# The down weights of sixteen experts in eight ring pieces of 2816 floats in place of eleven of 2048

## The reference, cut to what matters

```
D_MODEL = 1024
N_EXPERTS = 16
EC_CAPACITY = 2
D_FF = 128 * ((8 * D_MODEL // 3 + 127) // 128)    # 2816
```

## Time and profile before

| | |
|---|---|
| runs | 2968.31, 2967.54, 2962.93 us; median 2967.54 us |
| profiled execution | 2965.82 us, span 2964.0 us |
| TensorE matmuls | 2557.9 us busy, 86% of the span, 19787 instructions |
| TensorE weight loads | 1410.3 us busy, 48% |
| VectorE, ScalarE, GpSimd | 888.7, 413.0, 85.2 us busy |
| transfers | 789.18 MB, mean 266 GB/s |
| granted TensorE clock | 0.92 of full over the span |

### The profile page before, as it was taken

The page is one execution under the profiler, slowest core; times in us unless marked ns, Lnnn a source line. Parts: engine busy times, 40 slices in busy tenths (PEclk is TensorE's granted clock), DMA queues, the critical chain, the costliest instruction groups (busy, mean ns, idle before and its releaser), DMA issues. The chain is left out here.

```text
span 2964.0 us, 43931 instructions
## 1 busy us (share of the span) xinstructions
PE 2557.9 (86%) x19787; PEld 1410.3 (48%) x19787; DVE 888.7 (30%) x1788; ACT 413.0 (14%) x810; POOL 85.2 (3%) x93
## 2 busy tenths in 40 slices
PE   6979579988999998999999999879677889779995
PEld 4534235333344443544344443337565878445553
DVE  1216632201212212131303131026538441242222
ACT  1022100200101001021202121013113221000001
POOL 0001000000000000000000000000000200000000
PEclk9988688999999999999999999989878989889998
DMA  5316236799999998899988899863010005259996
GB/s 177 123 48 223 92 130 239 294 382 380 392 379 373 380 421 360 334 375 409 371 360 355 371 407 386 368 263 126 2 37 1 3 7 199 99 240 419 422 422 281
DMA packets 136340, 789.18 MB, mean 266 GB/s; under 512 B 18241, under 2 KB 20553, under 8 KB 65881
## 3 DMA queue, kind: packets, MB, share of 16 engines
q1 hardware_dynamic: 132697, 773.78, 64.9%
q0 software_dynamic: 3456, 12.58, 1.1%
HBM read 774.79 MB, written 11.53 MB: 265 GB/s over the span
## 5 line engine op out<-in xcount | busy, mean ns | idle before, releaser
L3015 PE MATMUL bank<-ring,arena 128*34 128x512 f32 (+1 forms) x3072 | 699.2, 595 | 105.1 <-DMA ring<-in_w_up 75.6
L3015 PEld LDWEIGHTS bank<-ring,arena 128*34 128x34 f32 x3072 | 185.0, 116 | 521.6 <-issue 506.9
L3037 PE MATMUL bank<-ring,arena 128*34 128x512 f32 x1408 | 320.5, 595 | 0.7 <-DVE arena L2021 0.6
L3037 PEld LDWEIGHTS bank<-ring,arena 128*34 128x34 f32 x1408 | 88.0, 112 | 178.2 <-issue 157.0
L303 PE MATMUL bank<-arena,ring 128*128 128x256 f32 (+1 forms) x688 | 158.7, 393 | 3.9 <-DVEq L2038 1.8
L303 PEld LDWEIGHTS bank<-arena,ring 128*128 128x128 f32 x688 | 133.8, 195 | 29.3 <-DVEq L2038 2.2
L3493 PE MATMUL bank<-ring,arena 128*64 128x256 f32 x992 | 111.3, 379 | 4.6 <-DMA ring<-in_moe_w_up 3.9
L2014 DVE TENSOR_TENSOR arena<-arena,bank 34x512 f32<-34x512 f32 x96 | 56.7, 646 | 152.6 <-ACT arena L1086 152.2
L2913 PEld LDWEIGHTS bank<-arena 64*64 64x64 f32 x2304 | 75.4, 139 | 52.6 <-issue 52.1
L313 PE MATMUL bank<-ring,arena 128*128 128x512 f32 (+1 forms) x224 | 98.8, 596 | 0.0
L3493 PEld LDWEIGHTS bank<-ring,arena 128*64 128x64 f32 x992 | 73.4, 137 | 46.3 <-issue 14.4
(11 more groups left out here) (634 smaller groups left out, 3003.6 us busy)
## 6 DMA issues: line engine op xcount, KB each, us to landing
ring<-in_w_gate SPq DMA_DIRECT2D x128, 1408.0 KB, 11.3
ring<-in_w_up SPq DMA_DIRECT2D x128, 1408.0 KB, 12.5
ring<-in_w_down SPq DMA_DIRECT2D x176, 1024.0 KB, 8.6
ring<-in_w_in SPq DMA_DIRECT2D x46, 1024.0 KB, 7.1
ring<-in_moe_w_down SPq DMA_DIRECT2D x33, 1024.0 KB, 15.8
ring<-in_moe_w_gate SPq DMA_DIRECT2D x31, 1024.0 KB, 14.3
ring<-in_moe_w_up SPq DMA_DIRECT2D x31, 1024.0 KB, 17.2
ring<-in_ada_w SPq DMA_DIRECT2D x24, 1024.0 KB, 6.6
```

What stands on the lines that cost most here:

```text
L3015: last = mm(ps[c][row:row + CAP, 0:n], xsT[:, e, k, :], w[:, at:at + n], start=k == 0, stop=k == KT - 1)
L3037: last = mm(ps[6][row:row + CAP, :], hidT[:, 2 * j + f, :], w[:, f, half * BANK:(half + 1) * BANK], start=j + f == 0, stop=j == FT // 2 - ...
```

## The change

The down weights of an expert go over in eight pieces of 2816 floats per partition, as large as a gate or up piece. Partition p now holds 22 consecutive rows of `w_down`, 22 p to 22 p + 21, and piece m is floats 2816 m to 2816 m + 2815 of that line of 22528. With this:

- `DOWN_AT` places eight pieces: one behind k = 2, 3, 5 and 7, two behind k = 4 and 6.
- The transposed hidden column g takes the hidden columns 22 p + g: a step of 22 floats.
- A piece holds 5.5 banks of 512 output columns, so half the piece ends fall in the middle of a bank, and that matmul is cut in two of 256 columns. An expert has 48 down matmuls in place of 44.
- In HBM a piece's 128 lines of 11264 bytes lie 90112 bytes apart. Before, a piece was one closed stretch of 1 MB.

```
-        DOWN_AT = {2: (0, 1), 3: (1, 3), 4: (3, 5), 5: (5, 7), 6: (7, 9), 7: (9, 11)}
-        hid_by2 = hid.rearrange("p (j q f) -> p j f q", q=P, f=2)
+        DOWN_AT = {2: (0, 1), 3: (1, 2), 4: (2, 4), 5: (4, 5), 6: (5, 7), 7: (7, 8)}
+        N_DOWN = FT * D // PIECE
+        hid_by22 = hid.rearrange("p (q j) -> p j q", j=FT)
...
-            for j in range(lo, hi):
-                w = A["w_down"][e][2 * j * P:(2 * j + 2) * P, :]
-                down_pieces[e].append(piece(w.rearrange("(p k) c -> p k c", k=2), 2 * D, "p (k c) -> p k c", {"k": 2}))
+            rows = A["w_down"][e].rearrange("(p j) c -> p (j c)", j=FT)
+            for m in range(lo, hi):
+                down_pieces[e].append(piece(rows[:, m * PIECE:(m + 1) * PIECE], PIECE, "p (o c) -> p (o c)", {"o": 1}))
...
-                    last = mm(ps[6][:, f * CAP:(f + 1) * CAP], hid_by2[0:CAP, g // 2, g % 2, :], ident[:CAP, :CAP],
+                    last = mm(ps[6][:, f * CAP:(f + 1) * CAP], hid_by22[0:CAP, g, :], ident[:CAP, :CAP],
...
-                for j in range(lo, hi):
-                    w, slot, count, _ = down_pieces[e][j]
+                for m in range(lo, hi):
+                    w, slot, count, _ = down_pieces[e][m]
                     pe.wait_ge(slot, count)
-                    for f in range(2):
-                        for row in (0, SLOT):
-                            half = row // SLOT
-                            last = mm(ps[6][row:row + CAP, :], hidT[:, 2 * j + f, :], w[:, f, half * BANK:(half + 1) * BANK],
-                                      start=j + f == 0, stop=j == FT // 2 - 1 and f == 1)
+                    at = m * PIECE
+                    while at < (m + 1) * PIECE:
+                        j, half, c = at // D, at % D // BANK, at % BANK
+                        n = min(BANK - c, (m + 1) * PIECE - at)
+                        row = SLOT * half
+                        last = mm(ps[6][row:row + CAP, c:c + n], hidT[:, j, :], w[:, at - m * PIECE:at - m * PIECE + n],
+                                  start=j == 0, stop=j == FT - 1)
+                        at += n
                     last.then_inc(piece_used, up(piece_used))
```

More of the change, by code:

```diff
@@ L531, in build @@
                         context_pieces[name] = column_pieces(A["w_in_2"], c0, cols)
-        add_down_pieces(N_EXP - 1, 0, FT // 2)
+        add_down_pieces(N_EXP - 1, 0, N_DOWN)
         n_experts = len(pieces)
@@ L3092, in _ @@
                 pe.wait_ge(hid_turned, due(pe, hid_turned))
-            down_pe(N_EXP - 1, 0, FT // 2)
+            down_pe(N_EXP - 1, 0, N_DOWN)
             pe.wait_ge(banks_read, due(pe, banks_read, 2))
```

## The result

The changed kernel takes 3063.82 us, the median of four runs (3056.98 to 3071.49), against 2967.93 us before: a ratio of 1.0323, 95% interval 1.0292 to 1.0354. It is slower, as forecast, but by 96 us and not by 53, and it lies just above the range of 2985 to 3062 us. The profiled execution took 3056.98 us with a span of 3055.0 us, 91.0 us more than before's.

What follows compares the result with a forecast made beforehand. Each expert was taken as a TensorE-bound part, then a transfer-bound part. +67.6 (transposes) - 27.9 (ring) + 0.9 (cuts) + 12.2 (clock) = +52.8 us on 2965.8 us gave 3018.6, with the runs' median 3020 us; range 2985 to 3062 us.

Steps and rivals of the forecast that it cites:

- the part that TensorE bounds: Each expert from k = 0 to the end of `gate_up_pe` of k = 2; work added here adds to the time in full.
- the ring's gain: At the k = 2 release the ring holds 0.786 MB more, 1.86 us less waiting per expert: -27.9 us over 15 experts.
- the part that the transfers bound: Each expert from the end of k = 2 until the next k = 0 pieces land; more TensorE work here is hidden.
- the transposes: Hidden-column transposes at step 22: 704 weight loads at 0.096 us more each, +67.6 us, bounds 0 and +84.5 us.
- the clock: Longer transpose groups make TensorE's clock fall more often, 1.63 us a fall: +12.2 us, bounds 0 and +48.9 us.
- the down products: Cut down matmuls hide in transfer waits, except in the last expert: +0.9 us, bounds 0 and +14 us.
- 0.117 and 0.213 us apart: Start spacing of successive transpose weight loads at steps 2 and 8, the latter taken for step 22: 0.096 us more per load.
- The signs named: In the changed profile, transpose loads near 313 ns median and a group of 22 about 4.8 us in place of 2.66.
- One further fall in every second expert: Clock falls behind transpose groups, counted as 15 x 0.5 x 1.63 = +12.2 us.
- the price per instruction: Down matmuls: 0.214 us per further instruction, lost only where two cut halves for the same rows meet.
- Scattered lines: Rival: down-piece lines 90112 bytes apart in HBM slow the transfers, +23 us, 3043 us in all; chance 0.07.
- The clock's rival: The clock falls behind every transpose group, up to +48.9 us, ending at 3057 us; chance 0.12.

Runs made afterwards that it cites:

- the ladder: The kernel before with its old pieces, its half groups of transposes taking steps of 1, 2, 3, 4, 8, 16 and 22 floats in turn: 3031.03 us, single run.
- Long groups of cheap loads: The kernel before with each transpose done twice at the old step of 2 floats: 3110.45 us, ratio 1.0475.
- The five slots: Kernel with eight pieces and the hidden tile stored in reading order, SP allowing five pieces instead of six in the experts' stage: 3008.7 us, ratio 1.0172.
- closed stretches: The changed kernel with each down piece read from one closed stretch of 1408 KB of w_down: 3061.35 us, ratio 1.0329.

## Why the prediction was right in sign and too small

The stage was read rightly: transposes in the part that TensorE bounds, the ring's gain in the part that the transfers bound, and the two add, as the two halves of the change run alone showed (+129 and -31 us for +96). The sum had three losses too small, the transposes, the clock and the down products, and the gain too small as well. On the profiled spans the miss is 91.0 - 52.8 = 38.2 us: 18.3 from the transposes, 19.2 from the down products and 11.5 from all other matmuls, less the 10.8 us by which TensorE's time without work fell further than the forecast had it (38.7 against 27.9).

- **The transposes: forecast +67.6 us, measured +85.9.** The step that failed is the spacing of slow loads, "0.117 and 0.213 us apart", taken from the first two of a sequence. Over 22 loads the spacing is 0.241 us. The bound of 0.120 us per load, +84.5 us, was nearly the answer. The signs named, a median of 313 ns and 4.8 us for the loads of a group, came out as 337 ns and 5.40 us. That a step of 22 costs what a step of 8 costs held in the ladder (0.245 and 0.241 us), and with it the rule of the Trainium skill (Advanced Engine Details and Errata, SBUF Cachelines) that one access per line is penalised and two are not. The cheaper step of 16 (0.220 us) isn't explained by it.
- **The clock: forecast +12.2 us, measured some +36 to +47 where the step is the only difference.** "One further fall in every second expert" failed. It was read from one expert, with one fall in two groups; before, 22 of the 32 groups have one, and now all 32, mostly longer. The work that the step doesn't touch grew by 47.2 us where the step came alone; with the new pieces it is 2169.8 us at step 22 against 2566.5 - 92.0 - 340.6 = 2133.9 us at step 2, +35.9 us. This was the forecast's own rival, with a chance of 0.12 and a price of up to 48.9 us. Long groups of cheap loads did the same (+43.4 us), so it was the length of the group that decided. Against before the growth is only 23.7 us, since the profile with new pieces and old step has fewer falls (18 of 32) and 12.2 us less of such work. These sums move between profiles: in the kernel with four cut matmuls the same sum is 2573.6 - 91.1 - 321.1 = 2161.4 us, 15 us above before without a cause in the code, so each is good to perhaps 15 us.
- **The ring: forecast -27.9 us, measured -31 us** for the new pieces alone, down products included. That the two lie so close is partly luck. In that profile TensorE's time without work fell by 36.4 us (406.1 to 2936.2 - 2566.5 = 369.7), while the down products took 20.1 us more and the other matmuls 12.2 us less. With the step of 22 the waits fell by 39.8 us, more than 27.9. The five slots bear out the arithmetic of the lead for the waits, 49.2 us for a piece less, not for the time.
- **The down products: forecast +0.9 us, measured +20.1 us of busy time.** The step that failed is the price per instruction, 0.214 us for each in turn, with a loss only where two cut halves meet. Four cut matmuls per expert with such meetings cost 0.6 us in all. The rows fit another count: the instructions of one half of the output rows run one after another, the two halves beside each other, and the fuller half sets the time. By the earlier trace rows one more instruction in each half costs (3.60 - 1.89) / 4 = 0.4275 us, with a tail of 1.89 - 1.71 = 0.18 us. A piece of 5.5 banks has three banks for one half and two and a half for the other, two instructions each. At k = 2 that is 6 x 0.4275 + 0.18 = 2.75 us (measured 2.74); at k = 4, with six banks against five, 5.31 us (5.32); at k = 6, where two pieces make 5.5 banks for each half, 4.88 us (4.89). Balanced, they would take 2.53, 4.88 and 4.88 us. Over k = 2 to 7 the excess is some 1.3 us an expert, 19 us over 15 experts, nearly all of the 20.1. No run changed the order within a piece alone, so this rests on the rows. The work lies in the transfer part, and the waits there gave up 11.9 us more than the lead explains (39.8 against 27.9); that the longer down products took these from them is an inference.
- **Scattered lines** were rightly held unlikely: 426 GB/s, and no difference with closed stretches.
- **The range** ended at 3062 us. With the sustained spacing (+85.9) and both falls (+48.9) the forecast's own terms would have given 2967.5 + 85.9 - 27.9 + 0.9 + 48.9 = 3075 us. The clock's rival was priced alone, on the forecast's transposes, though the two go together: a slower load is what makes the group longer.

## What to carry to other kernels

A layout that gives transfers one closed line can take it from the engine that reads across. Look at the step in floats of every operand loaded as weights, and where it passes two, turn the data on the write of an engine with time to spare. In a group of matmuls that is bound by its loads, count the slower load times all loads and then the clock behind the group: take them as one mechanism, not as two chances, and count falls of the clock over all groups, not in one example. Where matmuls alternate between two halves of output rows, sum each half by itself; the fuller one sets the time. With a ring of slots, what counts is the bytes that it holds when the transfers become the bound, so pieces of full slot size are worth their difference once per cycle.

## What the runs showed that was not expected

- A step of 4 floats costs already as much as one of 22 (0.236 and 0.245 us a load), and one of 16 less than one of 8 (0.220 and 0.241 us).
- The first spacing in a sequence of slow loads is 0.22 us and the sustained one 0.241 us.
- Slow loads don't follow the granted clock: a group of 22 takes 5.54 us at a mean of 0.96 and at 0.50 alike, where a group of cheap loads takes 2.78 us at 1.00 and 4.91 at 0.50.
- Two pieces of 5.5 banks behind each other take 4.89 us when the two halves of the output rows have 5.5 banks each, and 5.32 us when they have six and five.
- ScalarE's ACTIVATE and VectorE's TENSOR_TENSOR with a step of 128 floats in the hidden tile take 1056 and 1088 ns, against 552 and 646 ns before.
- A matmul of 512 columns cut in two of 256 adds nothing that shows, 321.1 against 320.5 us over 64 cuts.
